# Two setup programs of a decoder step made one: a single ring for both layers' modulation weights, and a pooling mixer by pairs of chunks

## The chip, the cores and the metric

The kernel runs on one core of a Trainium2 chip. A core has five engines that run their own instruction streams and meet at semaphores: TensorE (PE), VectorE (DVE), ScalarE (ACT), GpSimd (POOL) and SyncE (SP), which here issues nearly all DMA transfers; sixteen DMA engines carry them out. The metric is the device time of one execution in microseconds; a run with a profile also has a span, from the first to the last recorded instruction.

## The reference, cut to what matters

The kernel computes one step of a two-layer decoder over 1024 prompt rows and 64 sample rows (8 sequences of 8) of 1024 channels. The part around the change is the modulation of both layers and the first layer's mixer:

```python
def _ada(c, w, b):
    m = jax.nn.silu(c) @ w + b                      # w: 1024 x 6144, per layer
    return [t[:, None, :] for t in jnp.split(m, 6, axis=-1)]

def _pool_mixer(h, hist, pos0, w_pool, pool_scale):
    ...
    for g, w in enumerate(POOL_WINDOWS):            # windows 2, 4, 8, 16
        ...
        d = ((hi - lo) / cnt - extf[:, POOL_HIST:, sl]).astype(h.dtype)
        outs.append(d @ w_pool[g])                  # 256 x 256 per group
    out = jnp.concatenate(outs, axis=-1) * pool_scale
    return out, ext[:, -POOL_HIST:]

        sh1, sc1, g1, sh2, sc2, g2 = _ada(c, w_ada[layer], b_ada[layer])
        h = x * (1.0 + sc1) + sh1
        mix, hist = _pool_mixer(h, pool_hist[layer], pos0, w_pool[layer], pool_scale[layer])
        x = _layer_norm(DN_ALPHA * x + g1 * mix, ln_g[layer, 0], ln_b[layer, 0])
```

After it come the first layer's MLP, the shared keys and values, the second layer's attention (over a paged cache for the sample) and its MLP. The modulation is needed for nine rows of c: one of the prompt, eight of the sample.

## The kernel before

The program is a list of parts, one after the other, each a block of instruction streams with a barrier of all engines behind it: `setup`, `pool_mixer`, `first_layer_mlp`, `project`, `attend_sample`, `attend_prompt`, `second_layer_mlp`. The activations x_t lie in SBUF with channels on the partitions, in 8 chunks of 128 channels by 1088 columns (1024 prompt, 64 sample).

`setup` (line 99) loads c, the bias and norm vectors, and x, turns them on TensorE, and computes layer 0's modulation: the weight matrix w_ada (25.2 MB a layer) comes in 24 tiles of 128 rows by 2048 columns (1 MB) through a ring of four. SP issues a tile when the semaphore `ada_used` says that its slot is free (line 136); TensorE multiplies it by c (line 262) into four column groups of one bank; after each 8 tiles VectorE copies the sums (line 219), TensorE turns them (line 270), and `take_modulation` (line 79) adds the bias. `finish_modulation` (line 87) adds one to the scales and scales the gates.

`pool_mixer` (line 954) loads history, w_pool, and layer 1's weights in 48 tiles of 128 by 1024 (512 KB) through another ring of four (line 997). Per chunk of 128 channels ACT modulates the prompt's columns (line 1012). VectorE modulates the sample's (lines 1033 and 1034), builds the trailing sums by repeated shifted adds, for the prompt (line 1042) and the sample (line 1043), takes the difference (lines 1049 to 1056), and splits it into a high part (line 1057) and a low part (line 1059). TensorE multiplies both by w_pool in three products (`three`, lines 71 to 75), in pieces of 364, 364 and 360 columns, and VectorE adds the gated result to x (`gated_add`, line 276). Between the groups of two chunks TensorE works through 16 tiles of layer 1's modulation.

The order on each engine is the order of the code; each stream waits only at semaphores, in order.

Of the kernel before, what the change touches and what calls it, by code (L numbers as in the profile page):

```python
# [5 lines left out]
ALU = mybir.AluOpType  # L6
ACT = mybir.ActivationFunctionType
AX = mybir.AxisListType
# [76 lines left out]


def finish_modulation(dve, own, k, layer):

    m = k.mod[layer]
    for scale in (1, 4):  # L90
        own.mark(dve.tensor_scalar(m[:, 8 * scale:8 * scale + 8, :], m[:, 8 * scale:8 * scale + 8, :],
                                   1.0, None, ALU.add))
    for gate in (2, 5):
        own.mark(dve.tensor_scalar(m[:, 8 * gate:8 * gate + 8, :], m[:, 8 * gate:8 * gate + 8, :],
                                   1.0 / ALPHA, None, ALU.mult))
    own.settle()


def setup(nc, k, a):
    with ExitStack() as ctx:  # L100
        at = k.at
        x_rows = at("x_rows", [P, 9, D], F32, k.HH_AT)
        c_rows = at("c_rows", [P, D], F32, k.F_AT)
        c_e = at("c_e", [P, D], F32, k.F_AT + 4096)
        vec_rows = at("vec_rows", [P, 2, P], F32, k.F_AT + 8192)
        mod_rows = at("mod_rows", [P, 2, 512], F32, k.F_AT + 13312)
        w_raw = at("w_raw", [P, 4, 2048], F32, k.WORK_AT)
        ps = k.ps
        (x_in, c_in, v_in, made, x_turned, x_kept, x_free, c_done, c_turned, act_own, dve_own,
         ada_used, mod_kept, mod_turned, mod_out, v_turned, v_kept, b_in, z_set) = sems(  # L110
            ctx, nc, "set", "x_in", "c_in", "v_in", "made", "x_turned", "x_kept", "x_free", "c_done", "c_turned",
            "act_own", "dve_own", "ada_used", "mod_kept", "mod_turned", "mod_out", "v_turned",
            "v_kept", "b_in", "z_set")
        w_in = sems(ctx, nc, "set", "w_in0", "w_in1", "w_in2", "w_in3")
        block = ctx.enter_context(nc.Block())
        XJOBS = 18
        NIT = 3

        @block.sync
        def _(sp):  # L120
            sp.wait_ge(z_set, 2)
            sp.dma_start(c_rows[0:1, :], a["c_prompt"]).then_inc(c_in, 16)
            sp.dma_start(c_rows[1:9, :], a["c_sample"]).then_inc(c_in, 16)
            sp.dma_start(vec_rows[0:96, 0, :], a["b_ada"].rearrange("l (m p) -> (l m) p", p=P)).then_inc(v_in, 16)
            sp.dma_start(vec_rows[0:32, 1, :], a["ln_g"].rearrange("l s (m p) -> (l s m) p", p=P)).then_inc(v_in, 16)
            sp.dma_start(vec_rows[32:64, 1, :], a["ln_b"].rearrange("l s (m p) -> (l s m) p", p=P)).then_inc(v_in, 16)
            sp.dma_start(vec_rows[64:72, 1, :], a["pool_scale"].rearrange("l (m p) -> (l m) p", p=P)).then_inc(v_in, 16)
            sp.dma_start(k.bias_all[:, :], a["b_break"][0].partition_broadcast(P)).then_inc(b_in, 16)
            sp.dma_start(k.pages[:, :], a["page_table"].rearrange("b n -> (b n)").unsqueeze(0)).then_inc(b_in, 16)
            sp.dma_start(x_rows[:, 0:8, :], a["x_prompt"][0].rearrange("(t p) d -> p t d", p=P)).then_inc(x_in, 16)  # L130
            sp.dma_start(x_rows[0:TS, 8, :], a["x_sample"].rearrange("b t d -> (b t) d")).then_inc(x_in, 16)
            w = a["w_ada"][0].rearrange("(k p) n -> k p n", p=P)
# [4 lines left out]
            sp.wait_ge(b_in, 32)  # L137

        @block.gpsimd
        def _(pool):  # L140
            def made_by(ins):
                ins.then_inc(made, 1)
                made_by.n += 1
                pool.wait_ge(made, made_by.n)
            made_by.n = 0
            pool.memset(c_rows[:, :], 0.0).then_inc(z_set, 1)
            pool.memset(vec_rows[:, :, :], 0.0).then_inc(z_set, 1)
            made_by(pool.memset(k.ident[:, :], 0.0))
            made_by(pool.affine_select(out=k.ident[:, :], in_=k.ident[:, :], compare_op=ALU.not_equal, fill=1.0,
                                       base=0, pattern=[[-1, P]], channel_multiplier=1))  # L150
            made_by(pool.memset(k.mean_of[:, :], 1.0 / D))
            made_by(pool.memset(k.scratch[:, :], -1.0))

            made_by(pool.affine_select(out=k.scratch[:, :], in_=k.scratch[:, :], compare_op=ALU.is_ge, fill=0.0,
                                       base=0, pattern=[[-1, P]], channel_multiplier=1))
            made_by(pool.tensor_copy(k.neg_tri[:, :], k.scratch[:, :]))
            made_by(pool.memset(k.scratch[:, :], -1.0))
            made_by(pool.affine_select(out=k.scratch[:, :], in_=k.scratch[:, :], compare_op=ALU.is_gt, fill=0.0,
                                       base=0, pattern=[[1, P]], channel_multiplier=-1))
            made_by(pool.tensor_copy(k.neg_above[:, :], k.scratch[:, :]))  # L160

            made_by(pool.memset(k.scratch[:, :], 0.0))
            s3 = k.scratch[:, 0:TS]
            made_by(pool.affine_select(out=s3, in_=s3, compare_op=ALU.is_gt, fill=MASKED, base=0,
                                       pattern=[[1, TS]], channel_multiplier=-1))
            s3 = s3.rearrange("p (b q) -> p b q", q=DS)
            made_by(pool.affine_select(out=s3, in_=s3, compare_op=ALU.is_ge, fill=MASKED, base=0,
                                       pattern=[[-DS, DB], [0, DS]], channel_multiplier=1))
            made_by(pool.tensor_copy(k.mask_new[:, :], k.scratch[:, 0:TS]))
            made_by(pool.tensor_copy(k.ident_b[:, :], k.ident[:, :]))  # L170

            made_by(pool.memset(k.head_of[:, :], 1.0))
            made_by(pool.affine_select(out=k.head_of[:, :], in_=k.head_of[:, :], compare_op=ALU.is_ge, fill=0.0,
                                       base=0, pattern=[[-DS, H]], channel_multiplier=1))
            made_by(pool.affine_select(out=k.head_of[:, :], in_=k.head_of[:, :], compare_op=ALU.is_ge, fill=0.0,
                                       base=DS - 1, pattern=[[DS, H]], channel_multiplier=-1))

            for t in range(HIST):
# [1843 lines left out]
```

## Time and profile before

| what | value |
|---|---|
| median of 3 runs | 3507.91 us (3507.37 to 3510.8) |
| the profiled execution | 3508.96 us, span 3507.2 us |
| busy share of the span | PE 90%, PE weight loads 76%, DVE 56%, ACT 26%, POOL 13% |
| DMA | 433.92 MB, mean 124 GB/s |
| `setup` | 0 to about 91 us |
| `pool_mixer` | about 92 to 243 us |
| everything behind them | about 243.5 to 3507 us |

The busy share is a mean over parts with different limits. What the two first parts are limited by has to be read from their own stretch of the trace, as the section of rows does.

### The profile page before, as it was taken

The page shows a single profiled execution, that of the slowest core. Times are in us where ns is not written, and L with a number is a line of the kernel's source. Part 1 is how long each engine was busy: PE and PEld are TensorE (multiplying, and loading weights), DVE is VectorE, ACT ScalarE, POOL GpSimd, SP SyncE. Part 2 cuts the span into 40 slices and gives each one's busy share as a digit, 9 for nine tenths or more (in the row PEclk, how much of TensorE's full clock was granted, in tenths as well). Part 3 has the DMA queues.
Part 4 walks back from the last instruction along what each step waited for, and adds up shares of the span by engine and source line. Part 5 has one row for each costly group of instructions (what it writes and reads, how often), then busy time and mean ns, then how long its engine had stood idle before and what let it go on. Part 6 is the DMA issues. An engine that isn't in the chain of part 4 may idle for free. (4 is left out here: it accounts for less than half of the span.)

```text
span 3507.2 us, 55358 instructions
## 1 busy us (share of the span) xinstructions
PE 3171.7 (90%) x20656; PEld 2673.5 (76%) x20656; DVE 1963.4 (56%) x3447; ACT 926.8 (26%) x1610; POOL 439.0 (13%) x248
## 2 busy tenths in 40 slices
PE   5558999999998998799999997888799999999998
PEld 1237999999997998665656564444498999999996
DVE  2467555555556113366666666888726555555555
ACT  0114000000012002244444445777723000000003
POOL 0002211122111211000000000000021112212210
PEclk8879999999999998899999998999999999999999
DMA  8621111111110221499999993000021111111101
GB/s 340 240 96 48 44 36 36 36 48 43 46 49 29 80 66 48 150 402 408 409 407 407 407 406 113 25 24 20 12 61 31 37 37 48 43 47 48 48 25 51
DMA packets 215687, 433.92 MB, mean 124 GB/s; under 512 B 13664, under 2 KB 130057, under 8 KB 212441
## 3 DMA queue, kind: packets, MB, share of 16 engines
q1 hardware_dynamic: 215521, 431.67, 33.6%
q8 instruction: 109, 1.79, 0.2%
q14 instruction: 57, 0.47, 0.0%
HBM read 417.92 MB, written 13.92 MB: 123 GB/s over the span
## 5 line engine op out<-in xcount | busy, mean ns | idle before, releaser
L73 PE MATMUL bank<-hi,mlp_uphi 128*128 128x364 f32 (+1 forms) x1536 | 510.4, 332 | 16.1 <-DVE lo L417 6.2
L74 PE MATMUL bank<-lo,mlp_uphi 128*128 128x364 f32 (+1 forms) x1536 | 508.3, 331 | 0.0
L75 PE MATMUL bank<-hi,mlp_uplo 128*128 128x364 f32 (+1 forms) x1536 | 508.0, 331 | 0.0
L73 PE MATMUL bank<-mlp_fhi,mlp_dnhi 128*128 128x364 f32 (+1 forms) x1536 | 507.0, 330 | 0.1
L74 PE MATMUL bank<-mlp_flo,mlp_dnhi 128*128 128x364 f32 (+1 forms) x1536 | 504.8, 329 | 0.0
L75 PE MATMUL bank<-mlp_fhi,mlp_dnlo 128*128 128x364 f32 (+1 forms) x1536 | 504.7, 329 | 0.0
L290 DVE SCALAR_TENSOR_TENSOR x_t<-bank,mod,x_t 128x364 f32<-128x364 f32 (+1 forms) x432 | 245.2, 571 | 376.4 <-PE bank L75 374.3
L1589 PE MATMUL bank<-ident,sa_kraw 128*128 128x128 f32 x2048 | 276.8, 279 | 50.0 <-DMA sa_kraw<-in_cache_k 46.2
L73 PEld LDWEIGHTS bank<-hi,mlp_uphi 128*128 128x128 f32 x1536 | 291.6, 190 | 19.7 <-issue 17.8
L1589 PEld LDWEIGHTS bank<-ident,sa_kraw 128*128 128x128 f32 x2048 | 223.6, 141 | 103.1 <-DMA sa_kraw<-in_cache_k 74.1
L74 PEld LDWEIGHTS bank<-lo,mlp_uphi 128*128 128x128 f32 x1536 | 291.4, 190 | 0.3
L75 PEld LDWEIGHTS bank<-hi,mlp_uplo 128*128 128x128 f32 x1536 | 291.5, 190 | 0.0
L1471 DVE COPY sa_kt<-bank 128x512 f32<-128x512 f32 x256 | 177.0, 692 | 204.0 <-PE bank L1589 200.0
L73 PEld LDWEIGHTS bank<-mlp_fhi,mlp_dnhi 128*128 128x128 f32 x1536 | 288.7, 188 | 1.3 <-DVE mlp_flo L562 0.4
L74 PEld LDWEIGHTS bank<-mlp_flo,mlp_dnhi 128*128 128x128 f32 x1536 | 288.7, 188 | 0.9
L75 PEld LDWEIGHTS bank<-mlp_fhi,mlp_dnlo 128*128 128x128 f32 x1536 | 288.6, 188 | 0.0
L538 POOL TENSOR_TENSOR mlp_dnlo<-mlp_raw,mlp_dnhi 128x1024 fp32r<-128x1024 f32 x64 | 160.1, 2501 | 856.1 <-ACT mlp_dnhi L527 856.0
L527 ACT ACTIVATE mlp_dnhi<-mlp_raw 128x1024 fp32r<-128x1024 f32 x64 | 67.6, 1057 | 746.3 <-PE bank L75 656.6
L538 POOL TENSOR_TENSOR mlp_uplo<-mlp_raw,mlp_uphi 128x1024 fp32r<-128x1024 f32 x64 | 160.8, 2513 | 639.2 <-ACT mlp_uphi L527 400.3
L558 DVE TENSOR_SCALAR mlp_f<-bank 128x360 f32<-128x360 f32 (+1 forms) x192 | 102.0, 531 | 200.4 <-PE bank L75 200.1
L562 DVE TENSOR_TENSOR mlp_flo<-mlp_f,mlp_fhi 128x360 fp32r<-128x360 f32 (+1 forms) x192 | 209.3, 1090 | 6.6
L527 ACT ACTIVATE mlp_uphi<-mlp_raw 128x1024 fp32r<-128x1024 f32 x60 | 63.6, 1061 | 507.1 <-PE bank L75 410.6
(269 smaller groups left out, 5440.9 us busy)
## 6 DMA issues: line engine op xcount, KB each, us to landing
sa_kraw<-in_cache_k SPq DMA_DIRECT2D x256, 512.0 KB, 10.7
sa_vpage<-in_cache_v SPq DMA_DIRECT2D x256, 512.0 KB, 9.5
mlp_raw<-in_w_up SPq DMA_DIRECT2D x64, 512.0 KB, 4.0
mlp_raw<-in_w_down SPq DMA_DIRECT2D x64, 512.0 KB, 3.4
w_raw<-in_w_ada SPq DMA_DIRECT2D x24, 1024.0 KB, 8.6
pm_wada<-in_w_ada SPq DMA_DIRECT2D x48, 512.0 KB, 5.2
kv_raw<-in_w_kv SPq DMA_DIRECT2D x8, 1024.0 KB, 5.5
x_rows<-in_x_prompt SPq DMA_DIRECT2D x1, 4096.0 KB, 14.1
```

Source lines behind the costliest of these rows:

```text
L73: pe.matmul(out, w_hi, x_hi, start=start, stop=False, skip_group_check=True)
L74: pe.matmul(out, w_hi, x_lo, start=False, stop=False, skip_group_check=True)
L75: return pe.matmul(out, w_lo, x_hi, start=False, stop=stop, skip_group_check=True)
L290: dve.scalar_tensor_tensor(out=x, in0=psum[:, 0:wp], scalar=g[:, 8 * gate + m, 0:1], in1=x, op0=ALU.mult, op1=ALU.add).then_inc(free, 1)
L527: act.activation(self.split_target(kind, c)[0], self.raw[:, r % 2, :], ACT.Copy).then_inc(self.w_hi_done, 1)
L538: pool.tensor_tensor(lo, self.raw[:, slot, :], hi.bitcast(F32), ALU.subtract).then_inc(self.w_done, 1)
L558: own.do(dve.tensor_scalar(ft, u, 0.0, None, ALU.max))
L562: dve.tensor_tensor(self.f_lo[:, c, c0:c0 + w], ft, hi.bitcast(F32), ALU.subtract).then_inc(self.bank_free, 1)
L1471: dve.tensor_copy(k_t[:, 4 * h:4 * h + 4, P * g:P * g + P], TURN[job % 4][:, :].rearrange("p (c n) -> p c n", c=4)).then_inc(dve_kept, 1)
L1589: last = pe.transpose(TURN[job % 4][:, c * P:(c + 1) * P], k_raw[n % 2][:, g, (4 * h + c) * P:(4 * h + c + 1) * P], k.ident[:, :])
```

## The change

The two parts `setup` and `pool_mixer` become one, `entry`, with no barrier between them.

- SP issues x in four pieces of 1 MB, then the history, then the tiles of both layers' modulation weights, 96 of 512 KB, through one ring of eight slots. Bias, page table and the copy of the pool state inside DRAM are issued between the two layers. w_pool is loaded from POOL's queue at the start. The two memsets that SP waited for are gone.
- The silu of c is computed on the turned nine columns (72 elements a partition) instead of on rows of 1024.
- The mixer works by pairs of chunks: each VectorE operation covers 2 x 1088 columns. The high part is cast on ACT, the products are four of 512 columns and two of 64 for a group.
- The sample's modulation and trailing sums are computed on POOL, for all chunks at once, into two buffers; VectorE takes from them the difference alone. The history's copies go from VectorE to ACT.
- TensorE's order is written out: layer 0's first third, then the groups' products with stretches of tiles between them, the last at tile 72 of 96; the rows for the pool outputs are turned before the last eight tiles.

```diff
 def entry(nc, k, a):
+        RING = 8
+        ring = at("en_ring", [P, RING, 1024], F32, k.HH_AT + NC * T * 4)
         @block.sync
-            with sp.Fori(0, NIT) as it:
-                for c in range(NC):
-                    sp.wait_ge(ada_used, it * NC + (c + 1))
-                    sp.dma_start(w_raw[:, c % 4, :], w[c, :, bass.ds(it * 2048, 2048)]).then_inc(w_in[c % 4], 16)
+            for layer in range(2):
+                w = a["w_ada"][layer].rearrange("(k p) n -> k p n", p=P)
+                with sp.Fori(0, 3) as it:
+                    for r in range(2 * NC):
+                        sp.wait_ge(ada_used, it * (2 * NC) + (6 * NC * layer + r + 1))
+                        sp.dma_start(ring[:, r % RING, :], w[r // 2, :, bass.ds(it * 2048 + 1024 * (r % 2), 1024)]
+                                     ).then_inc(ada_in[r % RING], 16)
         @block.gpsimd
+            pool.dma_start(w_raw[:, :, :, :], a["w_pool"][0].rearrange("g (c p) n -> p g c n", p=P)).then_inc(w_in, 16)
+            pool.wait_ge(mod_ready, 1)
+            own.do(pool.tensor_tensor(new, k.x_t[:, :, TP:T].rearrange("p c (b t) -> p c b t", b=DB),
+                                      over(m[:, 8:16, 1:9], DS), ALU.mult))
+            own.do(pool.tensor_tensor(new, new, over(m[:, 0:8, 1:9], DS), ALU.add))
+            for g in range(4):
+                pool.tensor_tensor(to[:, 2 * g:8, :, lo:24], from_[:, 2 * g:8, :, lo:24],
+                                   from_[:, 2 * g:8, :, lo - step:24 - step], ALU.add).then_inc(sums_s, 1)
+                pool.wait_ge(sums_s, g + 1)
         @block.scalar
+            def high(g):
+                act.wait_ge(d_done, g + 1)
+                if g >= 2:
+                    act.wait_ge(mixed, 5 * (g - 1))
+                act.activation(x_hi[:, g % 2, :, :], d[:, :, :], ACT.Copy).then_inc(hi_done, 1)
         @block.vector
+            def difference(g):
+                dve.wait_ge(h_done, g + 1)
+                own.mark(dve.tensor_copy(tail_p[:, 2 * g:2 * g + 2, :], hp[:, :, HW - HIST:HW]))
+                while step < win:
+                    to = s_p[:, n % 2, :, :]
+                    own.do(dve.tensor_tensor(to[:, :, lo:HW], src[:, :, lo:HW], src[:, :, lo - step:HW - step], ALU.add))
+                    src, step, n = to, 2 * step, n + 1
+                    lo += step
...
+                dve.wait_ge(sums_s, g + 1)
...
+            def low(g):
+                dve.wait_ge(hi_done, g + 1)
+                if g >= 2:
+                    dve.wait_ge(mixed, 5 * (g - 1))
+                dve.tensor_tensor(x_lo[:, g % 2, :, :], d[:, :, :], x_hi[:, g % 2, :, :].bitcast(F32), ALU.subtract
+                                  ).then_inc(lo_done, 1)
...
         @block.tensor
+            modulation(0, every)
+            turn_modulation(0)
+            modulation(1, every[:12])
+            mix(0)
+            modulation(1, every[12:])
+            modulation(2, every[:4])
+            turn_modulation(1)
+            modulation(2, every[4:10])
+            mix(1)
...
+            modulation(5, every[8:])
+            turn_modulation(5)
```

On TensorE the tiles of weights and the first products stand as follows before the change (bank is PSUM, w_raw and pm_wada are the two rings, c_t is c, pm_whi and pm_wlo are w_pool's high and low part, hi the difference's high part):

```order
L262 MATMUL bank<-w_raw,c_t 32x512 x32
L270 MATMUL bank<-ident,mod_rows 128x128 x4
L100 UNCONDITIONAL_BRANCH
L1086 UNCONDITIONAL_BRANCH
L1090 MATMUL bank<-ident,pm_hist 128x120 x8
L1102 MATMUL bank<-pm_wada,c_t 32x512 x32
L73 MATMUL bank<-hi,pm_whi 128x364
```

And this is TensorE's stream at the same place in the changed program (en_ring is the one ring, x32 are 16 tiles of it):

```order
L1118 MATMUL bank<-ident,en_hist 128x120 x8
L1134 MATMUL bank<-en_ring,c_t 32x512 x32
L1144 MATMUL bank<-ident,en_modrows 128x128 x4
L1134 MATMUL bank<-en_ring,c_t 32x512 x24
L73 MATMUL bank<-en_xhi,en_whi 128x512
L74 MATMUL bank<-en_xlo,en_whi 128x512
```

The barrier (the branches) is gone, the history is turned ahead of the first tile, and the first product stands behind 28 tiles of 512 KB, not behind all of layer 0's and 16 of layer 1's.

On VectorE one chunk of the mixer is this before (pm_hs is the sample's, pm_hp the prompt's modulated input, pm_ss and pm_sp their sums, pm_d the difference):

```order
L1030 COPY pm_hs<-bank 128x8x15
L1033 TENSOR_TENSOR pm_hs<-x_t,mod_61 128x8x8
L1034 TENSOR_TENSOR pm_hs<-pm_hs,mod_61 128x8x8
L1035 COPY pm_ts<-pm_hs 128x64
L1037 COPY pm_tp<-pm_hp 128x15
L1042 TENSOR_TENSOR pm_sp<-pm_hp 128x1039
L1043 TENSOR_TENSOR pm_ss<-pm_hs 128x8x23
L1049 SCALAR_TENSOR_TENSOR pm_d<-pm_sp,pm_hp 128x1023
L1051 SCALAR_TENSOR_TENSOR pm_d<-pm_ss,pm_hs 128x64
L1057 CAST hi<-pm_d 128x1088
L1059 TENSOR_TENSOR lo<-pm_d,hi 128x1088
```

After the change VectorE's stream has for the first pair of chunks, behind the first third of the modulation:

```order
L994 TENSOR_SCALAR mod_61<-mod_61 128x72
L1011 COPY en_tailp<-en_hp 128x30
L1014 TENSOR_TENSOR en_sp<-en_hp 128x2x1039
L1020 SCALAR_TENSOR_TENSOR en_d<-en_sp,en_hp 128x2x1023
L1023 TENSOR_TENSOR en_d<-en_sp,inv_seen 128x2
L1027 SCALAR_TENSOR_TENSOR en_d<-en_ss_76,en_hs 128x64 x2
L1031 TENSOR_TENSOR en_d<-en_d,en_hp 128x2
L1038 TENSOR_TENSOR en_xlo<-en_d,en_xhi 128x2176
```

Half as many instructions, each over two chunks; the sample's copies, modulation and sums and the high part's cast have left this stream.

POOL had nothing behind its constants before; now its stream goes on like this in the same part:

```order
L894 MEMSET en_hs 128x64
L900 TENSOR_TENSOR en_hs<-x_t,mod_61 128x64x8
L902 TENSOR_TENSOR en_hs<-en_hs,mod_61 128x64x8
L906 TENSOR_TENSOR en_ss_76<-en_hs 128x64x23
L906 TENSOR_TENSOR en_ss_81<-en_ss_76 128x48x21
L906 TENSOR_TENSOR en_ss_76<-en_ss_81 128x32x17
L906 TENSOR_TENSOR en_ss_81<-en_ss_76 128x16x9
L912 COPY en_tails<-en_hs 128x512
```

These are 512, 512, 1472, 1008, 544 and 144 elements a partition with two inputs each, and a copy of 512.

## Rows read from the trace of the kernel before

**Rows 1.** Windows over the part before the MLP: busy us and instructions, clock, DMA.

```profile
0.00:92.00 92.00, 46.61 (x286) 16.40 (x286) 19.77 (x32) 7.51 (x11) 7.25 (x38) 0.86 0.82 324
92.00:108.00 16.00, 2.15 (x10) 1.68 (x12) 6.71 (x15) 4.17 (x3) 0.00 (x0) 0.50 0.56 172
108.00:202.00 94.00, 69.59 (x307) 25.46 (x304) 53.51 (x111) 7.45 (x6) 0.00 (x0) 0.91 0.73 258
202.00:243.50 41.50, 11.48 (x59) 10.55 (x57) 28.63 (x62) 0.00 (x0) 0.00 (x0) 0.67 0.03 8
sum 243.50, PE 129.82 PEld 54.09 DVE 108.62 ACT 19.13 POOL 7.25; mean PE 32.46 PEld 13.52 DVE 27.16 ACT 4.78 POOL 1.81
```

**Rows 2.** Windows with full DMA engines: setup, mixer, page cache; last column GB/s.

```profile
51.00:56.00 5.00, 2.13 (x16) 0.32 (x16) 0.00 (x0) 0.00 (x0) 0.00 (x0) 1.00 1.01 421
...
123.00:124.00 1.00, 0.75 (x4) 0.00 (x0) 0.00 (x0) 0.00 (x0) 0.00 (x0) 1.00 1.04 385
...
1600.00:1650.00 50.00, 45.57 (x435) 29.62 (x428) 29.79 (x56) 22.08 (x39) 0.00 (x0) 1.00 1.03 408
```

**Rows 3.** DMA issues: size of each, median us from issue to landing.

```profile
pm_wada<-in_w_ada SPq DMA_DIRECT2D x48, 512.0 KB, 5.2
x_rows<-in_x_prompt SPq DMA_DIRECT2D x1, 4096.0 KB, 14.1
```

**Rows 4.** Timeline, end of setup and the first instruction of the mixer.

```profile
85.53 1.62 PE L262 MATMUL bank<-w_raw,c_t 128*32 128x512 f32 x8 [0.66 <-DMA w_raw<-in_w_ada]
87.22 0.69 DVE L219 COPY mod_rows<-bank 128x512 f32<-128x512 f32 x1 [19.01 <-PE bank L262]
...
91.92 0.09 DVE L1018 MEMSET pm_hp<- 128x32 f32 x1 [1.50 <-PEq L43]
```

**Rows 5.** Timeline, end of the mixer and start of the MLP.

```profile
238.09 0.70 SPq L1002 DMA_DIRECT2D out_pool_sample<-pm_os  x1
...
243.56 0.23 DVE L366 TENSOR_TENSOR coef<-mod,vec_t 128x72 f32<-128x72 f32 x1 [5.50 <-PEq L43]
```

**Rows 6.** Timeline, start of the program: x is issued, and TensorE gets it.

```profile
5.15 0.40 SPq L130 DMA_DIRECT2D x_rows<-in_x_prompt  x1
...
21.36 9.73 PE L251 MATMUL bank<-ident,x_rows 128*128 128x128 f32 x72 [5.73 <-DMA x_rows<-in_x_sample]
```

**Rows 7.** Groups by line and shape, 0 to 241 us: busy us, mean ns of one.

```profile
L1042 DVE TENSOR_TENSOR pm_sp<-pm_hp 128x1039 f32<-128x1039 f32 x8 | 9.9, 1233 | 0.0
L1012 ACT ACTIVATE pm_hp<-x_t,mod 128x1024 f32<-128x1024 f32 x8 | 9.8, 1238 | 79.7 <-DVE hi L1057 79.7
L290 DVE SCALAR_TENSOR_TENSOR x_t<-bank,mod,x_t 128x364 f32<-128x364 f32 x16 | 9.5, 597 | 8.0 <-PE bank L75 7.7
...
L1049 DVE SCALAR_TENSOR_TENSOR pm_d<-pm_sp,pm_hp 128x1023 f32<-128x1023 f32 x2 | 2.4, 1224 | 0.1
```

**Rows 8.** Timeline in the first MLP: VectorE beside POOL.

```profile
312.98 2.36 POOL L538 TENSOR_TENSOR mlp_dnlo<-mlp_raw,mlp_dnhi 128x1024 fp32r<-128x1024 f32 x1 [59.40 <-ACT mlp_dnhi L527]
314.27 1.45 DVE L559 TENSOR_TENSOR mlp_f<-mlp_f 128x360 f32<-128x360 f32 x1
315.29 2.63 POOL L538 TENSOR_TENSOR mlp_uplo<-mlp_raw,mlp_uphi 128x1024 fp32r<-128x1024 f32 x1
...
315.76 2.37 DVE L561 CAST mlp_fhi<-mlp_f 128x360 fp32r<-128x360 f32 x1
...
318.16 0.54 DVE L562 TENSOR_TENSOR mlp_flo<-mlp_f,mlp_fhi 128x360 fp32r<-128x360 f32 x1
```

**Rows 9.** Timeline of TensorE in the mixer: tiles of weights, and a mix.

```profile
139.46 1.92 PE L1102 MATMUL bank<-pm_wada,c_t 128*32 128x512 f32 x16
144.75 4.58 PE L1102 MATMUL bank<-pm_wada,c_t 128*32 128x512 f32 x12 [3.37 <-DMA pm_wada<-in_w_ada]
...
165.03 0.43 PE L73 MATMUL bank<-hi,pm_whi 128*128 128x364 f32 x1
...
171.10 0.60 PE L1112 MATMUL bank<-ident,pm_modrows 128*128 128x128 f32 x4
```

More of the change, by code:

```diff
@@ new lines, in _ @@
+            keep_modulation(0)
+            take(0)
+            difference(0)
+            low(0)
+            difference(1)
+            keep_modulation(1)
+            low(1)
+            take(1)
+            gated(0)
+            difference(2)
+            keep_modulation(2)
+            low(2)
+            take(2)
+            gated(1)
+            difference(3)
+            low(3)
+            gated(2)
+            keep_modulation(3)
+            gated(3)
+            take(3)
+            dve.wait_ge(b_in, 32)
@@ L1096, in modulation @@
[L1096 to L1104 removed]
+                if c % 4 == 3:
+                    last.then_inc(hist_turned, 1)
@@ new lines, in _, with modulation @@
+            pe.wait_ge(c_done, 1)
+            def modulation(n, tiles):
+                bank = ADA[n % 2]
+                for r in tiles:
+                    if r == 0:
+                        if n == 1:
+                            pe.wait_ge(hs_kept, 2)
+                        if n >= 2:
+                            pe.wait_ge(mod_kept, n - 1)
+                    pe.wait_ge(ada_in[r % RING], 16 * (2 * n + r // RING + 1))
+                    for q in range(2 * (r % 2), 2 * (r % 2) + 2):
+                        last = pe.matmul(bank[32 * q:32 * q + 32, :], k.c_t[:, r // 2, :],
+                                         ring[:, r % RING, 512 * (q % 2):512 * (q % 2) + 512], start=(r < 2),
+                                         stop=(r >= 2 * NC - 2), tile_position=(0, 32 * q), skip_group_check=True)
@@ L1132, in _ @@
-            pe.wait_ge(tails, 1)
-            pe.wait_ge(mod_out, 3)
-            for rows, tail, bank in ((HIST, tail_p, 4), (TS, tail_s, 6)):
+            every = range(2 * NC)
+            modulation(0, every)
[7 more added lines that the diff above has]
+            mix(1)
+            modulation(2, every[10:])
@@ new lines, in _ @@
+            modulation(3, every[:4])
+            turn_modulation(2)
+            modulation(3, every[4:12])
+            mix(2)
+            modulation(3, every[12:])
+            modulation(4, every[:8])
+            mix(3)
+            modulation(4, every[8:12])
+            turn_modulation(3)
+            modulation(4, every[12:])
+            modulation(5, every[:4])
+            turn_modulation(4)
+            modulation(5, every[4:8])
+            pe.wait_ge(tail_done, 1)
+            pe.wait_ge(d_done, 4)
@@ L1135, in _ @@
+            pe.wait_ge(freed, 20)
+            for rows, tail, bank in ((HIST, tail_p, 0), (TS, tail_s, 2)):
                 for c in range(NC):
@@ L1983, in build @@
     steps = [
-        lambda: setup(nc, k, a),
-        lambda: pool_mixer(nc, k, a),
+        lambda: entry(nc, k, a),
         lambda: first_layer_mlp(nc, k, a),
```

560 lines of the change are left out of this document (266 added, 294 removed).

## The prediction

> **What bounds the kernel now.** I read the windows first, cut where the program changes its work [rows 1]. The matmuls of the later parts fill the span, but the change touches only the first 243.6 us, in which TensorE is busy for 130 us. Up to 92 us the DMA engines are 0.82 busy and move 324 GB/s; from 92 to 108 us they do half of that; from 108 to 202 us 258 GB/s; from 202 to 243.5 us they are idle, while VectorE is busy for 28.6 of 41.5 us. So this stretch is a chain of two loads of weights with work between them that nothing covers. Its bytes are 2 x 25.2 MB of modulation weights, 4.5 MB of x, 1.0 MB of w_pool and 0.5 MB of history: 56.3 MB.
>
> What the transfers can do stands in three windows [rows 2]: 421 GB/s in setup (rows of 8 KB, four transfers of 1 MB asked for at a time), 408 GB/s over the page cache (transfers of 512 KB, rows of 4 KB), and in the mixer 385 GB/s in a microsecond in which the engines were full, though its ring of four gets only 258 GB/s on the mean. That ring is short, not the engines slow: a transfer of 512 KB takes 5.2 us from issue to landing [rows 3], the matmuls on it (4.58 us for three tiles at most, 1.92 for four at best [rows 9]) about 1.1, and four in flight every 6.3 us are 1.57 us a tile.
>
> The end of a stage costs as follows. In setup the matmuls on the last tile start at 85.53 us, the copy of the sums at 87.22, and the first instruction of the next part on VectorE at 91.92 [rows 4]: 6.4 us, of which some 0.9 is work on small constants that the change moves elsewhere. The mixer's last store is issued at 238.09 and the next part begins at 243.56 [rows 5]; it is that 243.6 which the new part has to beat.
>
> **The change part by part.** The time of the part up to the MLP becomes, if loads bound it: start of the ring's bytes, plus 96 tiles of 512 KB, plus stalls, plus the way from the last tile to the next part.
>
> Start. In before, x is issued at 5.15 us (behind two memsets of POOL that SP waits for, six small loads, and bias and pages), it lands 14.1 us later [rows 3], and TensorE gets the sample's rows, queued behind it, at 21.36 [rows 6]. Now SP waits for nothing and bias and pages come later, so x is issued some 2 us earlier. History (0.5 MB) is queued ahead of the ring, and w_pool (1 MB, on POOL's queue) shares the engines from the first microseconds, ahead of x's bytes. Both are 1.5 MB, 3.6 us at 421 GB/s, partly hidden in the gap at the start. The ring's bytes begin at 19.5 us; bounds 18.5 and 21.
>
> Tiles. 524,288 bytes take 1.245 us at 421 GB/s, 1.285 at 408, 1.36 at 385. Eight tiles in flight are 10.4 us of transfer, over the 6.3 us of one tile's way round, so the engines stay full. The nearest row in shape (4 KB, 512 KB) is the cache's, the nearest in address the 385; I take 1.30 us, so 124.8 us. The worst reading is the ring of four as a whole: 258 GB/s at a busy share of 0.73 would be 354 GB/s at a share of one, 1.48 us a tile and 142 us.
>
> Here a page speaks against the change. The Trainium skill (DMA: Bandwidth & Descriptors, section Bandwidth) counts about 358 GB/s of HBM for each core of a pair when both stream, and wants transfers of 1 MiB or more. By it a tile would take 1.46 us. The 421 and 408 GB/s of this core alone [rows 2] are over that figure.
>
> Also in the queue between the layers: the copy of the pool state inside DRAM, bias and pages, 0.5 MB moved in all: 1 us.
>
> Mixer on VectorE. A pair of chunks doubles each operation's elements. 1.23 us for 1039 and 1.22 for 1023 [rows 7] give 2.3 us for an add or a difference over a pair, 2.45 for the low part, 0.77 for a gated add of 512 columns from the 0.60 of 364. The cast to the high part goes from VectorE to ACT: 2 us for 2176 elements, by its 1.24 for 1024 [rows 7]. The four pairs need 1, 2, 3 and 4 adds: VectorE has 23 + 9.2 + 9.8 + 14.7 (gated) + 8 (copies and modulation) + 3 (small) = 68 us of work after the first third of modulation. That ends by 43.6 + 68 = 112 us, and the last tile lands at 150. The whole mixer therefore hides beside layer 1's loads, which is where the gain is: in before the loads for layer 1 start only behind setup, and the last pair's 41.5 us are bare [rows 1].
>
> The first mix on TensorE decides if the ring stalls. Tile 16 lands at 19.5 + 20.8 = 40.3 us; matmul, copy, transposes, add and plus one take 3.3 us [rows 4], so the modulation is ready at 43.6. Then ACT modulates a pair (2.5), VectorE sums (0.2 + 2.3 + 2.3 + 0.9), ACT casts (2.0), VectorE subtracts (2.45): 13.0 us with the handovers. TensorE is through its 12 further tiles 13.3 us after the modulation: just in time. Behind the waiting mix stand all further tiles on TensorE, behind those SP's issues.
>
> **But POOL.** The sample's sums move from VectorE to POOL. In the MLP, POOL's two-input operation over 1024 takes 2.4 us, and VectorE's work beside it stretches until POOL is done [rows 8]: a square that ends at 315.7 instead of 314.8, a cast over 360 elements that takes 2.37 us and ends 0.2 us after POOL's, and 0.54 us for the like once POOL is quiet. The Trainium skill says the same of the shared SBUF interface (GPSIMD Engine Reference, section Specifications: contention with VectorE instructions that have two SBUF inputs). At 2.35 ns an element POOL needs 1.2 + 1.2 us for the sample's modulation (beside ACT), then 3.4, 2.3, 1.3 and 0.4 for the sums. Taken in turn with VectorE's adds these delay the first pair by at least 3.1 us (the first sum) and at most 7.8 (all, and the tail's copy); I take 6. TensorE waits 6, and mixes for 6.4: 36 matmuls of about 364 columns took 165.03 to 171.10 us [rows 9], so 24 of 512 take 5.7 and twelve of 64 some 0.7. With 3 us more (1.1 for the first tile, and of the 5.2 us from issue to landing [rows 3] some 2 before bytes flow, an estimate) that is 15.4 us, against 10.4 us in flight: a stall of 5 us. Were the mix in time, 9.4 us: no stall. At the later mixes the chain has room: 14, 18 and 12 tiles (18.2, 23.4, 15.6 us) stand between the mixes, and VectorE needs about 15, 17 and 18.5 us; the third is 3 us over, which the slack of the second returns.
>
> End. The last third of layer 1 goes the way that setup's goes [rows 4]: 6.4 - 0.9 = 5.5 us to the next part. The stores and tail transposes stand in front of the last eight tiles, hidden by their 10.4 us; without that cover the last store alone would cost the 5.5 us from 238.09 to the next part [rows 5].
>
> Sum: 19.5 + 124.8 + 1 + 5 + 5.5 = 155.8 us instead of 243.6, a gain of 87.8. The profiled run took 3508.96 us for a span of 3507.2, the median of the runs shown is 3507.91, 1 us below. From the median: 3420 us. What comes after is not touched.
>
> The shorter path of c (exp and reciprocal over 72 elements instead of 1024) gains nothing of itself: TensorE waited for x until 21.36 us all the same [rows 6].
>
> **The rivals.**
> - *Rows of 4 KB load slowly*: 1.48 us a tile, 142 us, so 3437 us. For: the 258 GB/s at a share of 0.73. Against: 408 GB/s over the cache. By the Trainium skill's 358 GB/s (the page above) it would be 3436. Chance 0.13.
> - *The mixes stall the ring each time*: the pairs' chain is late at all four mixes, 5 us each, 15 more: 3435 us. For: POOL's sums come in turn. Against: they are done after the second pair. Chance 0.09.
> - *TensorE at its lower level.* Twelve matmuls of three tiles once took 4.58 us, where sixteen of four took 1.92 [rows 9]. At 1.2 GHz throughout, 80 tiles of 0.96 us (twice the 0.48), four mixes of 12 (not quite twice the 6.4) and some 8 us of transposes are 133 us from 43.6 us on, then 5.5: 182 instead of 155.8, 3446 us. The granted clock is 0.86 and 0.91 over the two long windows [rows 1], so only stretches would be slow. Chance 0.04.
> - *Slower than before*: the ring's transfers hinder each other until a tile takes longer than (243.6 - 19.5 - 1 - 5 - 5.5) / 96 = 2.21 us, 237 GB/s. The ring of four as a whole is at 258, near it, but each further transfer in flight would have to take rather than give. At 2.3 us it would be 3517. Chance 0.01.
> - *No effect*: bytes are the same, so the stretch would keep its length only if the average of 234 GB/s over it were a limit; windows of 421 speak against. Chance 0.01.
>
> **How the numbers follow.** My forecast (the ring bounds, one stall) has 0.72 and 3409 to 3430: the low end is 1.245 us a tile, no stall, and an early start (5.3 + 5 + 1), the high end 1.36 us and a second stall. The range takes in the slow rows: 3409 to 3437. Faster by over 0.2% (about 7 us, what a measurement of this kernel can tell from none) 0.98, same 0.01, slower 0.01.
>
> **What would show it.** Right: one stretch of 400 GB/s or more from about 5 to 150 us, with one dip near 60 to 70 us; the first mixing matmul near 63 us; the first VectorE add longer than 2.3 us beside POOL; the MLP's first instruction near 156 us. Wrong: a steady 350 GB/s; TensorE's tile matmuls waiting for VectorE instead of DMA past 80 us; a part after 156 us that takes another time than before.

## The result, and the profile after

The changed kernel takes 3452.91 us (median; 3451.13 to 3456.33 over 4 runs), beside 3509.36 us for the kernel before in the same series: a ratio of 0.9839, 95% interval 0.9826 to 0.9851. The forecast was 3420 us with a range of 3409 to 3437: the direction was right, the gain (56 us) is well short of the 88 us forecast. The profiled execution took 3456.33 us for a span of 3454.6 us.

Windows of the changed kernel, over the new part and over the middle of the page cache (columns as in [rows 1]: busy us and instructions of PE, PEld, DVE, ACT and POOL, granted clock, DMA share, GB/s):

```profile
0.00:15.00 15.00, 6.21 (x35) 5.89 (x36) 3.41 (x9) 2.72 (x4) 7.10 (x38) 1.00 0.83 305
15.00:20.00 5.00, 4.22 (x39) 3.98 (x38) 3.14 (x5) 2.79 (x5) 0.00 (x0) 1.00 1.04 301
20.00:46.00 26.00, 19.55 (x90) 4.36 (x87) 4.17 (x5) 4.40 (x12) 0.00 (x0) 1.00 1.03 399
46.00:64.00 18.00, 11.59 (x49) 1.60 (x48) 13.26 (x11) 8.93 (x7) 12.89 (x7) 0.95 1.03 410
64.00:80.00 16.00, 14.42 (x76) 9.05 (x76) 12.03 (x16) 4.29 (x3) 0.00 (x0) 0.85 0.45 162
80.00:110.00 30.00, 25.58 (x124) 9.20 (x124) 21.71 (x28) 2.02 (x1) 0.00 (x0) 1.00 0.98 382
110.00:155.00 45.00, 38.59 (x198) 16.71 (x196) 21.53 (x30) 2.02 (x1) 0.00 (x0) 0.92 0.90 335
155.00:172.40 17.40, 10.81 (x56) 3.14 (x56) 3.77 (x8) 0.00 (x0) 0.00 (x0) 0.97 0.60 240
1480.00:2046.00 566.00, 509.24 (x4860) 331.98 (x4849) 347.67 (x680) 240.69 (x425) 12.38 (x24) 1.00 1.02 399
```

Two things stand in it. The ring runs at 410 GB/s from 46 to 64 us, against 258 for the ring of four in [rows 1], but then it falls to 162 and stays below 400 for the rest of the part: it stalls. And the page cache, which the change does not touch, moves 399 GB/s where the same 566 us of the kernel before moved 407:

```profile
1546.00:2112.00 566.00, 520.86 (x4986) 338.97 (x4975) 355.93 (x697) 245.87 (x436) 12.38 (x24) 1.00 1.03 407
```

The end of the part, in the timeline of the changed kernel (the rows that answer to [rows 4, 5]):

```profile
166.74 1.05 PE L1134 MATMUL bank<-en_ring,c_t 128*32 128x512 f32 x4 [0.19 <-DMA en_ring<-in_w_ada]
...
167.84 0.69 DVE L983 COPY en_modrows<-bank 128x512 f32<-128x512 f32 x1 [7.06 <-PE bank L1134]
...
172.44 0.23 DVE L177 TENSOR_TENSOR coef<-mod,vec_t 128x72 f32<-128x72 f32 x1 [2.52 <-PEq L43]
```

The MLP begins at 172.44 us instead of 243.56: 71.1 us gained where 87.8 were forecast. But the span is only 52.6 us shorter, so 18.5 us are given back behind 172.44, where the forecast said that nothing is touched. There are two errors to explain, 16.6 and 18.5 us. Comparing the same VectorE instructions in both traces shows where the second lies (the page part is counted from its first to its last VectorE instruction). The MLP starts 71.1 us earlier, the page part 66.4 us earlier, and its end is only 52.5 us earlier, as is nearly everything after it. The page part gives back 13.9 us, and what lies ahead of it 4.7.

### The profile page after: what moved, and what is told of

Same layout as the page of the kernel before. It is cut to its first block and busy times, and to the rows that moved or that the text cites. A ratio compares the mean times of both kernels' runs of the same rounds, so it can differ in the third digit from the quotient of the medians.

```text
span 3454.6 us, 55334 instructions
## 1 busy us (share of the span) xinstructions
PE 3174.5 (92%) x20656; PEld 2675.0 (77%) x20656; DVE 1937.2 (56%) x3338; ACT 936.7 (27%) x1622; POOL 452.7 (13%) x255
## 3 DMA queue, kind: packets, MB, share of 16 engines
q0 software_dynamic: 272, 1.05, 0.1%
## 5 line engine op out<-in xcount | busy, mean ns | idle before, releaser
L101 DVE SCALAR_TENSOR_TENSOR x_t<-bank,mod,x_t 128x364 f32<-128x364 f32 (+1 forms) x408 | 231.7, 571 | 367.9 <-PE bank L75 366.2
```

Source lines behind the costliest of these rows:

```text
L101: dve.scalar_tensor_tensor(out=x, in0=psum[:, 0:wp], scalar=g[:, 8 * gate + m, 0:1], in1=x, op0=ALU.mult, op1=ALU.add).then_inc(free, 1)
```

## The experiments

The theories at the start: for the time given back, **A** (it belongs to the changed program; as A1 to the transfer on POOL's queue, as A2 to something else in it) and **B** (it is chance). For the ring, **C** (a mix stalls it by the length of its pause).

**The changed kernel once more**, no edit.

> The changed kernel as it is, a second time, to tell a lasting cost from a chance one. In its first trace the new part ends 71.1 us earlier than the two old parts did (172.4 against 243.6 us), but only 52.6 us of that are left at the end: the paged cache's loads take 709 us instead of 695, at 384 to 394 GB/s instead of 406, and other places give back some 4 us. If the slower cache loads belong to the program (theory A), this trace again shows them at 385 to 396 GB/s and a time near 3453 us. If they were chance (theory B), they are at 405 to 408 GB/s and the time is near 3440 us.

Measured: 3451.67 us, ratio 0.9832 (0.9816 to 0.9848). The page part starts 68.0 us earlier than in the kernel before and ends 53.7 us earlier: it gives back 14.3 us again. B falls.

Here the MLP begins at 170.97 us. Three kernels further below have the same code up to the MLP and differ only in padding behind it; there it begins at 171.76, 169.54 and 169.05 us. So the 172.44 us of the trace that I explain is the latest of five, and between single traces a difference of up to some 3 us in this part says little.

**w_pool on SP's queue**, and the reverse, the kernel before with it on POOL's.

```
-            pool.dma_start(w_raw[:, :, :, :], a["w_pool"][0]...)
+            sp.dma_start(w_raw[:, :, :, :], a["w_pool"][0]...)     # ahead of the ring
```

> The changed kernel with w_pool issued from SP, behind the history and ahead of the ring, instead of from POOL. Theory A1: one transfer from POOL's queue makes every later transfer a little slower (4 KB packets took 168 ns instead of 163 in the cache part), so without it the cache part returns to 695 us and the whole is some 13 us faster than the changed kernel, near 3440 us. Rival A2: the slower packets come from something else (the layout of the code in memory, instruction fetches, which are 98 packets instead of 70 on one queue): the cache part stays near 709 us and the time within 3 us of 3453. In the new part the bytes ahead of the ring are the same, so tile 0 should land near 23 us either way.

> The kernel before with this one edit: w_pool is issued from POOL's queue, in the mixer's part. Theory A1 (a transfer from POOL's queue slows all later ones): the cache part takes 709 us instead of 695 and the whole is some 13 us slower, near 3522 us. Rival A2: no difference beyond 2 us, since w_pool itself is waited for in the same place (landing 6.4 us after issue in the changed kernel).

Measured: 3452.79 us, 0.9836 (0.982 to 0.9852), with the page part slow as before; and 3510.18 us, 1.0002 (0.9993 to 1.0012), with it quick. A1 falls on both sides.

**A tile between the products of a mix.** Each mix is cut behind each of its four large products, with one tile's matmuls in between.

```
                     product(ps[j][:, :], c, slice(512 * half, 512 * half + 512)).then_inc(mixed, 1)
+                    if between:
+                        modulation(n, between[j:j + 1])
```

> The changed kernel with each mix cut up on TensorE: behind each of its four products of 512 columns stands one tile of weights that stood behind the mix. Nothing else moves. Theory C: the ring stalls whenever TensorE leaves it alone for longer than about 6.2 us (tile 28 to 35 are in flight when the mix begins, and the next must be issued about a microsecond before they have landed), and each mix takes 6.9 to 9.2 us; the landings of the 96 tiles lie 143.7 us apart where 95 intervals of 1.28 us would be 121.6, so 22 us of stalls. Split, the pauses are 1.5 to 3 us (5.5 for the first, with VectorE late by 4): stalls fall below 6 us and the new part ends 14 to 18 us earlier, near 156 us, for a time near 3437 us. Rival D: what slows the ring is VectorE's chain (gated adds and low parts late), not the length of a mix: then TensorE waits inside the split mixes and the part ends less than 6 us earlier. Rival E: SP's issue of 0.58 us a tile behind a mix is what costs: the splits spread it, same sign as C, but the stalls behind the first mix alone would stay as they are.

Measured: 3449.3 us, 0.9825 (0.9808 to 0.9841); the MLP begins at 169.96. That is 2.5 us earlier, not 14 to 18, and inside the spread of the unedited part: C in this form falls, and 19.1 us of stalls are left by the landings. Rival D's time came true (less than 6 us earlier), but not its cause: TensorE waits for VectorE in front of the first mix (4.30 us), but not inside the split ones. The trace says why the split does not help. TensorE's tiles between two products, in the first mix:

```profile
70.61 1.05 PE L1134 MATMUL bank<-en_ring,c_t 128*32 128x512 f32 x4
...
73.19 1.05 PE L1134 MATMUL bank<-en_ring,c_t 128*32 128x512 f32 x4
```

A product of six matmuls and one tile take 2.58 us together (73.19 less 70.61), and a tile lands every 1.28 us when the ring flows. TensorE falls behind its tiles all the same, only in steps. SP asks for the next tiles at 69.13, 71.84, 74.42 and 77.00 us, each behind TensorE's matmuls on a tile, so its 0.58 us an issue (rival E) is not what paces the ring there.

**Where the page part's time goes.** By now I had looked at SP, which issues the page loads, instruction by instruction. At each of the six jumps back of the loop over the sequences, the keys of the next sequence are issued late. Timeline of SP in the kernel before, at such a jump:

```profile
1702.99 1.81 SPq L1326 DMA_DIRECT2D sa_vpage<-in_cache_v  x4
1706.09 4.09 SPq L1317 DMA_DIRECT2D sa_kraw<-in_cache_k  x4
```

and in the changed kernel:

```profile
1639.69 1.86 SPq L1389 DMA_DIRECT2D sa_vpage<-in_cache_v  x4
1647.76 4.06 SPq L1380 DMA_DIRECT2D sa_kraw<-in_cache_k  x4
```

Between them lie the instructions of the loop's own line; the view of that line in the changed kernel (count, duration in ns, first and last start in us):

```profile
L1394 SPq COMPARE_BRANCH  x1: 53/53/53, 1641.7 to 1641.7; - x1
L1394 SPq FUSED_REGOPS  x1: 68/68/68, 1646.9 to 1646.9; - x1
```

The branch takes 53 ns, and the next instruction, a register operation that waits for nothing, starts 5.2 us later. In the kernel before it is 0.3 us (0.2 from the end of the branch):

```profile
L1331 SPq COMPARE_BRANCH  x1: 45/45/45, 1704.9 to 1704.9; - x1
L1331 SPq FUSED_REGOPS  x1: 68/68/68, 1705.2 to 1705.2; - x1
```

Six jumps make 31 us of such gaps, and the page part is longer by 14 only; that the loads already in flight hide the rest is my reading. The queue list counts packets of instructions: 57 on one queue in the kernel before, 87 in the changed one.

```profile
q14 instruction: 87, 0.71, 0.1%
```

The same list over the gap alone, from 1641.7 to 1646.9 us, has one of them:

```profile
q14 instruction: 1, 0.01, 0.4%
```

In each of the six gaps such a packet starts 3.5 us behind the branch; in the kernel before none starts within 6 us of a jump. So SP waits at each jump for code that is fetched anew. The page loop has 350 instructions on SP, and the change had moved it, unaltered, 30 instructions further into SP's program. That can be tried alone: increments of an unused semaphore, where SP waits for tens of us anyway (behind the last weight load of the first MLP).

```
             ff.sync(sp)
+            for _ in range(226):        # 30 in the kernel before; 98 and 60 further below
+                sp.sem_inc(pads, 1)
```

> The changed kernel with 226 increments of an unused semaphore on SP, behind its last weight load of the first MLP, where it waits for tens of us anyway. Nothing of the computation is changed. They move the code of all later loops of SP by 226 instructions; the changed kernel had moved them by 30 against the kernel before, so that the page loop's code now stands 256 instructions from its old place. Theory A2 (the code of SP's page loop lies badly: at each of its six jumps back the next instruction comes 5.2 us late, against 0.2 us before): the gap after the jump is 0.3 us or less, the cache part takes about 692 us instead of 706, and the time is 3439 us (3436 to 3443). Rival A3 (the page loads are slow for another reason, and the jump is late only because something else is): the gap and the part stay, 3452 us.

> The kernel before with 30 such increments at the same place, which puts the code of SP's page loop as many instructions into the program as in the changed kernel. Nothing of the computation is changed. Theory A2: the gap after each of the six jumps back becomes 5.2 us, the cache part 706 us instead of 692, the time 3523 us (3519 to 3526). Rival A3: 3510 us, as the kernel before.

Measured: 3438.59 us, 0.9797 (0.978 to 0.9813), and 3524.10 us, 1.0045 (1.0028 to 1.0061). Both went as A2 said. In the changed kernel with 226 more the jump costs 0.3 us and the keys follow the values as in the kernel before:

```profile
1635.03 1.86 SPq L1391 DMA_DIRECT2D sa_vpage<-in_cache_v  x4
1638.19 4.04 SPq L1382 DMA_DIRECT2D sa_kraw<-in_cache_k  x4
```

The kernel before, otherwise unchanged, has the gap with 30 more:

```profile
1707.46 1.79 SPq L1328 DMA_DIRECT2D sa_vpage<-in_cache_v  x4
1715.45 4.06 SPq L1319 DMA_DIRECT2D sa_kraw<-in_cache_k  x4
```

Its page part gives 13.6 us back, and its q14 counts 87 packets; the padded changed kernel's counts 59.

**One matmul of the six in each product** (the output then lacks the other five, the low parts and half the contraction).

```
-                    for q in range(2):
-                        last = three(pe, out, ..., q == 0, q == 1)
-                    return last
+                    return pe.matmul(out, w_hi[:, g, 0, ...], x_hi[:, g % 2, 0, cols], start=True, stop=True, ...)
```

> The changed kernel with one of the six matmuls of each product of the mixes (it leaves out the second half of the contraction and the low parts). Theory C2 (the ring stalls by what a mix keeps TensorE longer than the tiles in flight last, and by nothing else): each mix takes 1.5 us or less, the last tile lands near 152 us instead of 166.7, the next part begins near 158, and the time is 3438 us (3435 to 3442). Rival D (the loads stall for another cause, such as the small transfers between the layers, or SP's issues): the last tile lands after 160 us, 3446 us or more.

Measured: 3436.49 us, 0.9794 (0.9778 to 0.981). The last tile's matmuls:

```profile
150.66 1.05 PE L1134 MATMUL bank<-en_ring,c_t 128*32 128x512 f32 x4 [0.19 <-DMA en_ring<-in_w_ada]
```

They start at 150.66 instead of 166.74, and the MLP at 156.37. The mixes' time on TensorE is what stalls the ring; the small transfers between the layers cost 1.8 us here, and all stalls together 5.3 (22.1 in the changed kernel), by the landings in the trace.

**No sample sums on POOL** (left out of the result; zeros are written early in their place).

> The changed kernel without the sample's modulation and running sums on POOL; it writes zeros there before the modulation is ready, and this part of the result is left out. Theory P (POOL delays VectorE, VectorE the first mix, and the wait halves TensorE's clock in it): VectorE's first add takes 2.3 us instead of 4.8, the first mix begins near 60 us and takes 7 us instead of 9.2, of the 8.3 us of stall at it some 5 go, and the time is 3447 us (3444 to 3450). Rival: the mix is late for another reason or the ring loses the same later, 3452 us.

Measured: 3446.05 us, 0.9817 (0.9801 to 0.9834). In the changed kernel the first pair's sums on VectorE lie beside POOL's:

```profile
46.83 1.08 POOL L900 TENSOR_TENSOR en_hs<-x_t,mod 128x512 f32<-128x512 f32 x1 [36.35 <-DVE mod L994]
...
49.15 2.64 POOL L906 TENSOR_TENSOR en_ss<-en_hs 128x1472 f32<-128x1472 f32 x1
51.86 7.64 POOL L906 TENSOR_TENSOR en_ss<-en_ss 128x1008 f32<-128x1008 f32 x3
...
49.19 4.78 DVE L1014 TENSOR_TENSOR en_sp<-en_hp 128x2078 f32<-128x2078 f32 x1
54.00 3.84 DVE L1020 SCALAR_TENSOR_TENSOR en_d<-en_sp,en_hp 128x2046 f32<-128x2046 f32 x1
...
64.03 2.32 DVE L1014 TENSOR_TENSOR en_sp<-en_hp 128x2078 f32<-128x2078 f32 x1
```

The same add takes 4.78 us beside POOL and 2.32 once POOL is quiet, at 64.03. Without POOL's sums it takes 2.32 at once, in this kernel's timeline:

```profile
49.51 2.32 DVE L1003 TENSOR_TENSOR en_sp<-en_hp 128x2078 f32<-128x2078 f32 x1
51.86 2.29 DVE L1009 SCALAR_TENSOR_TENSOR en_d<-en_sp,en_hp 128x2046 f32<-128x2046 f32 x1
```

The first mix then starts at 60.14 us without a wait. In the changed kernel it waits:

```profile
64.18 0.77 PE L73 MATMUL bank<-en_xhi,en_whi 128*128 128x512 f32 x1 [4.30 <-DVE en_xlo L1038]
64.74 0.63 PE L74 MATMUL bank<-en_xlo,en_whi 128*128 128x512 f32 x1
65.17 0.63 PE L75 MATMUL bank<-en_xhi,en_wlo 128*128 128x512 f32 x1
```

Behind those 4.3 us of idleness its matmuls follow each other by 0.43 us, later by 0.23: the lower clock level, 1.2 GHz, and then the full 2.4. The window from 60 to 70 us has a granted clock of 0.66; without POOL's sums, and so without the wait, it has 1.00. The mix takes 9.2 us instead of 6.9. What the pause does to the ring stands in the changed kernel's timeline around the mix:

```profile
58.82 1.05 PE L1134 MATMUL bank<-en_ring,c_t 128*32 128x512 f32 x4 [0.23 <-DMA en_ring<-in_w_ada]
...
73.31 3.64 PE L1134 MATMUL bank<-en_ring,c_t 128*32 128x512 f32 x32
...
78.52 1.05 PE L1134 MATMUL bank<-en_ring,c_t 128*32 128x512 f32 x4 [0.98 <-DMA en_ring<-in_w_ada]
```

TensorE leaves the ring alone from 59.87 to 73.31 us, then finds eight tiles landed and works them off, and then waits for the next, which could be asked for only after 73.31.

**The first mix four tiles later.**

```
-            modulation(1, every[:12])
+            modulation(1, every)
             mix(0)
-            modulation(1, every[12:])
```

> The changed kernel with the first mix four tiles later in TensorE's order, behind all 16 tiles of that third instead of 12. Nothing of the computation is changed. Theory P (TensorE stands for 4.3 us in front of the first mix, at a lower granted clock behind it, because VectorE is late beside POOL): the four tiles take the place of the wait, the mix takes 7 us instead of 9.2, the stall at it falls from 8.9 us to 3, the last tile lands near 161 us instead of 166.7, and the time is 3447 us (3444 to 3450). Rival: VectorE's later work (the sums' release, the second pair) moves back with the mix and the later mixes lose what the first gains, 3452 us.

Measured: 3444.63 us, 0.9811 (0.9796 to 0.9826); the first mix starts at 65.70 without a wait and at the full clock, and the MLP begins at 165.95. This gains as much as leaving out POOL's sums, 7 to 8 us against the two medians of the changed kernel, and keeps the whole computation. In neither of the two runs does the clock record go to its lower level in the first mix, and TensorE does not wait in front of it.

**A product for every two tiles, and the padding.**

```
+            for g, at_tile in enumerate((30, 44, 60, 74)):
+                for j, t in enumerate((0, 2, 4, 6, 7)):
+                    plan.setdefault(at_tile + t, []).append(("mix", g, j))
+            for t in range(88):
+                modulation(t // 16, (t % 16,))
+                for kind, g, j in plan.get(t + 1, []): ...
```

> The changed kernel with each mix cut into its four large products and the sample's, one large product behind every second tile of the ring (first from tile 30 on, then 44, 60 and 74), and the 226 increments on SP. Nothing of the computation is changed. Theory C3 (what stalls the ring is how far TensorE falls behind its tiles, with 6 us to spare; one product and one tile take 2.58 us where a tile lands every 1.28, so a product for each tile still falls behind, a product for every two tiles hardly): stalls of 4 to 7 us in all instead of 22.6, the last tile lands near 150 us, the next part begins near 156, and with the 13.5 us of the page loop the time is 3423 us (3418 to 3428). Rival (the mixes cost the ring their TensorE time however they are laid): no better than one product for each tile, 3436 us.

Measured: 3421.17 us (5 runs), ratio 0.9743 (0.973 to 0.9757), the best of all. TensorE's timeline in a mix:

```profile
65.79 1.06 PE L1136 MATMUL bank<-en_ring,c_t 128*32 128x512 f32 x8
66.79 0.50 PE L73 MATMUL bank<-en_xhi,en_whi 128*128 128x512 f32 x1
...
68.37 1.07 PE L1136 MATMUL bank<-en_ring,c_t 128*32 128x512 f32 x8
```

A product with two tiles takes 2.58 us, what a product with one took, and two tiles land in 2.56. The window that moved 162 GB/s now moves 385, and the MLP begins at 154.80 us, with 3.7 us of stalls in all by the landings:

```profile
64.00:80.00 16.00, 15.50 (x96) 7.44 (x96) 14.27 (x20) 4.29 (x3) 0.00 (x0) 1.00 0.99 385
```

**Two more places for SP's loop.**

> The changed kernel with 98 such increments instead of 226, which puts the page loop of SP 128 instructions from its old place instead of 256. Nothing of the computation is changed. If the place counts in steps of 128 instructions: 0.2 us at each jump back, 3439 us. If only in steps of 256, or if what counts is the distance to the end of a larger block: another gap, 3439 to 3453 us.

> The changed kernel with 60 such increments, which puts SP's page loop 90 instructions from its old place. Nothing of the computation is changed. Theory L (SP's code comes in blocks of 128 instructions; the loop of 350 lies in three of them or in four, by its place; in three the block that the jump goes back to is still there, in four it must be fetched again; the places 0, 128 and 256 have three, 30 has four): at 90 it lies in four, the gap at each jump back is 5.2 us, the page part 706 us, the time 3452 us (3449 to 3455). Rival (30 is a place of its own, such as one where the jump stands at the end of a block, and most places are quick): the gap is 0.2 us, 3438 us.

Measured: with 98 more, 0.2 us at the jump and 3436.57 us, 0.9791 (0.9776 to 0.9806); with 60 more, 5.2 us and 3454.34 us, 0.9838 (0.9818 to 0.9858). Their page parts take 696.3 and 713.1 us, 3 us more than in the kernel before and in the changed one with 226 more (693.2 in both), and 3 to 6 more than in the other slow ones (706.7 to 710.5; forecast 706); why is not shown. Against the place in the kernel before, 0, 128 and 256 are quick, 30 and 90 slow (and in the two kernels with w_pool moved, -1 is quick and 31 slow). That is what blocks of 128 instructions would give, where a loop of 350 lies in three blocks or in four. But blocks of 256 would give it too, where the loop lies in two or in three: for either size there are places of the loop in the program for which all these runs come out as they did. A shift of 160 would tell them apart and was not run. What speaks for 128 is that the packets on q14 carry 8 KB each and come one at a time, which fits, if an instruction has 64 bytes; I have not shown that size. The Trainium skill (Runtime: NRT & Kernel Launch, section Instruction fetch mechanics) states that a taken branch to code outside a window of two blocks of 16 KiB, 256 instructions each, stalls until the block is fetched. The runs agree with the stall and give it 5.2 us; they leave 256 as the step possible, and only the 8 KB of SP's packets speak against 16 KiB blocks there.

## Why the prediction was wrong, step by step

- **What bounds the part, and the tile's time: right.** A tile lands every 1.28 us while the ring flows, 410 GB/s, against the 1.30 taken. Over 96 tiles this gives 1.9 us back. It is again over the 358 GB/s that I had weighed from the Trainium skill (DMA: Bandwidth & Descriptors, section Bandwidth), which are for two cores streaming at once, while one core runs here; and the rival of 1.48 us a tile falls.
- **Start of the ring's bytes: 2.3 us too early.** The first tile landed at 23.04 us, so its bytes stand for a start of 21.8, not 19.5. From 15 to 20 us the engines are full (1.04) but move only 301 GB/s. The modulation was ready at 46.65, not 43.6. Which of the transfers is slow there was not tried.
- **The mixes: the step that failed.** I had allowed one stall of 5 us and written of the others "were the mix in time, 9.4 us: no stall". The ring stood still for 22.1 us in all beyond its 1.28 us a tile, against 6 allowed (1 and 5). By the landings in the trace: 9.2 at the first mix, 3.1 at the change of layers just behind the second, 4.2 and 3.5 at the third and fourth, and the rest at the start and the tail's transposes. The first mix was late as forecast (the wait was 4.3 us, not 6), but it then ran for 9.2 us and not 6.4, at the lower clock level behind the wait (6.9 at the full one). The other three were in time, took 6.9, 7.0 and 7.2 us, and still stalled. I had set a pause of mix plus 3 us against the 10.4 us of eight tiles in flight, a margin of 7.4 us. But when TensorE is done with a tile the next has all but landed: at the first mix that is at 59.87 us, and the last tile asked for lands at 68.92, 9.0 us (7 x 1.28) later. The way from issue to landing is 3.9 us at the shortest:

```profile
DMA to landing us min/median/max: 3.9/9.0/18.4
```

That makes a margin of 5.0 us at best, and the stalls of the third and fourth mix leave 2.8 and 3.7. The rival "the mixes stall the ring each time" was nearly the case, for another reason than it gave: the chain of the pairs was in time from the second on. That the mixes are the cause the run with one matmul of six shows, by 16 us; that a pause must not only be cut but spread until TensorE keeps up, the runs with one tile and with two tiles between the products.

- **POOL: right, but the clock was left out.** VectorE's sum and difference took 4.78 and 3.84 us beside POOL, 4.0 us more than alone (2.32 and 2.29); I had taken 6, within 3.1 to 7.8. The lower clock behind the wait stood nowhere in my sum. All that hangs on POOL (the wait, the clock, the stall) is worth some 6 to 8 us by the medians, against the 5 of the one stall that I had allowed: without POOL's sums the MLP begins at 165.27 us, with the mix four tiles later at 165.95, instead of 172.44.
- **The end: right.** 5.7 us from the last tile's matmuls to the MLP, forecast 5.5.
- **"What comes after is not touched": wrong.** No instruction there was changed, but SP's were moved, and 13.9 us of the 18.5 come from six jumps of one loop. I had set this term at nothing, since no instruction there was edited. The padding takes the gaps away in the changed kernel and makes them in the kernel before, so the cause is shown.
- The other 4.7 us lie ahead of the page part: 3.6 in the first MLP and 1.1 behind it. Those in the MLP come in steps: 1.1 us in its first 8 us, 0.8 between 314 and 324 us (times of the kernel before), none over the next 740 us, and 1.7 in the norm at its end. That last step is one wait of VectorE for TensorE, in the kernel before and in the changed one:

```profile
1068.27 3.25 DVE L376 TENSOR_TENSOR x_t<-x_t,bank 128x1456 f32<-128x1456 f32 x2 [3.60 <-PE bank L344]
1000.75 3.25 DVE L187 TENSOR_TENSOR x_t<-x_t,bank 128x1456 f32<-128x1456 f32 x2 [5.29 <-PE bank L155]
```

The granted clock there is 1.00 before (1061 to 1070 us) and 0.79 in the changed kernel (989.9 to 998.1 us), and over the first 8 us of the MLP 0.78 and 0.64. The kernel before with w_pool on POOL's queue, which has no part of this change, takes the same three steps (3.6 us in all, clock 0.64 over the first 8 us). All runs of the changed kernel and its variants lose 0.9 to 3.8 us over the first MLP, and the kernel before with 30 increments 1.6. So most of it may be chance; what decides it stays open.

Two of the recorded sums are off by one in the last place: 2.3 us a tile gives 3516 us, not 3517, and the high end of the forecast 3431, not 3430. Nothing hangs on either.

Both errors point the same way. The sum by its own steps: 2.3 - 1.9 + 16.1 + 0.2 = 16.7 us, of the 16.6 in the part, and 18.5 behind it. Either alone would have left the time near the end of the range; the two together put it 16 us outside. With the mixes spread and the loop at its quick place the MLP begins at 154.80 us (forecast 155.8) and the kernel takes 3421.17 us: the ring can give what the forecast counted on, the change as made does not take it.

## What to carry to other kernels

Here a ring of eight hid a pause of its consumer only up to 3 to 5 us: the 9.0 us of seven tiles still to land, less the 3.9 us of the shortest way from issue to landing. Work the same difference out for another ring from its own trace. So spread foreign work until its share fits into each tile's interval, rather than trust the depth. Work that starts an engine's chain shouldn't lie beside POOL's sums, which took VectorE's add from 2.32 to 4.78 us here. A wait of TensorE can cost its clock as well: the wait of 4.3 us did, one of 1.74 us in front of the first product of the spread kernel did not (granted clock 1.00). When a part that was not edited becomes slower, look at the gaps behind branches in the loops of the engine that issues the loads: a shift of code alone can cost what an edit elsewhere gains.

## What the hardware showed that I had not expected

A jump back in a loop of 350 instructions on SP costs 0.2 us or 5.2 us by the loop's place in the program, steady over all six jumps in each of nine traces at slow places (5.1 to 5.3) and five at quick ones (0.2 to 0.3). One tile of weights added to a product costs TensorE's order as much as two tiles, 2.58 us for either: a tile alone takes 1.05 us, two in a row 1.06.
